# One decoder layer in fp32: transfers of the attention turns issued by slots, and an eighth block-product pair

## The reference

```
h = rms_norm(x, g_pre_mix)
cb, cc, ch, q, k, v, ga, gb = split(h @ w_in)     # 512 x 6, then 1024 x 2 columns
y_a = (cb * causal_dwconv(cc * ch)) @ w_a
o = stick_breaking(q, concat(k_past, k), concat(v_past, v), sb_bias)   # 8 heads of 64
y_b = o @ w_b
x = x + rms_norm((sigmoid(ga) * y_a + sigmoid(gb) * y_b) @ w_o, g_post_mix)
```

## Time and profile before

| what | us |
|---|---|
| median of three runs | 1709.57 |
| the profiled execution | 1707.09 |
| its span, first to last instruction | 1705.4 |
| PE busy | 1659.8 |
| DVE busy | 1177.9 |
| ACT busy | 828.0 |
| POOL busy | 361.3 |

### The profile page before, as it was taken

How to read it: one execution, slowest core, us unless ns; L and a number is a source line. 1 busy time by engine, 2 the same in 40 slices (tenths; PEclk the granted TensorE clock), 3 DMA queues, 4 the chain that set the end, 5 groups by cost and what they waited for, 6 DMA issues and landing times.

```text
span 1705.4 us, 25989 instructions
## 1 busy us (share of the span) xinstructions
PE 1659.8 (97%) x8721; PEld 1428.5 (84%) x8721; DVE 1177.9 (69%) x1669; ACT 828.0 (49%) x1430; POOL 361.3 (21%) x292
## 2 busy tenths in 40 slices
PE   9899998989999999999999999999999999999998
PEld 8688887978788889998878888888888888888886
DVE  7865525636366355665878888888888698777566
ACT  7322245747466455224564444444444444465675
POOL 1244300000000000000126666666665100000100
PEclk9899999999999999999999999999999999999999
DMA  5112233222213412444322222222221863244333
GB/s 179 47 43 76 93 100 90 73 78 68 85 53 100 165 58 102 154 142 154 110 69 80 78 77 78 77 77 78 77 78 57 284 234 100 82 149 172 121 128 118
DMA packets 180042, 178.33 MB, mean 105 GB/s; under 512 B 17999, under 2 KB 144811, under 8 KB 179948
## 3 DMA queue, kind: packets, MB, share of 16 engines
q1 hardware_dynamic: 167706, 170.54, 30.8%
q10 hardware_dynamic: 12242, 6.58, 1.3%
HBM read 133.56 MB, written 43.52 MB: 104 GB/s over the span
## 4 chain that ended last, share of the span: by engine, by line
PE 68%; DVE 1%; ACT 1%; SPq 1%; issue 0%; DMA 0%; POOL 0%; DVEq 0%; ACTq 0%; POOLq 0%
PE pair L3729 10%; PE pair L3789 8%; PE pair L3791 8%; PE pair L3790 8%; PE pair L3927 4%; PE pair L3928 4%; PE pair L3929 4%; PE pair L3798 2%; PE pair L3222 2%; PE pair L3272 2%; PE pair L3274 2%; PE pair L3273 2%; PE pair L3199 2%; PE pair L3197 2%; PE pair L3198 2%; PE pair L3592 1%
## 5 line engine op out<-in xcount | busy, mean ns | idle before, releaser
L3272 PE MATMUL pair<-xh,wh 128*128 128x384 f32 (+1 forms) x600 | 208.2, 347 | 1.1 <-DVE kl L2542 1.1
L3274 PE MATMUL pair<-xh,wl 128*128 128x384 f32 (+1 forms) x600 | 198.1, 330 | 0.0
L3273 PE MATMUL pair<-xl,wh 128*128 128x384 f32 (+1 forms) x600 | 198.1, 330 | 0.0
L1249 POOL TENSOR_TENSOR hn<-hn 128x512 f32<-128x512 f32 x4 | 5.2, 1292 | 646.0 <-DVE hn L2751 646.0
L3927 PE MATMUL pair<-woph,foph 128*128 128x512 f32 x308 | 120.4, 391 | 0.0
L3929 PE MATMUL pair<-woph,fopl 128*128 128x512 f32 x308 | 119.9, 389 | 0.0
L3928 PE MATMUL pair<-wopl,foph 128*128 128x512 f32 x308 | 119.9, 389 | 0.0
L3272 PEld LDWEIGHTS pair<-xh,wh 128*128 128x128 f32 x600 | 115.3, 192 | 4.9 <-issue 3.2
L3273 PEld LDWEIGHTS pair<-xl,wh 128*128 128x128 f32 x600 | 114.8, 191 | 0.0
L3274 PEld LDWEIGHTS pair<-xh,wl 128*128 128x128 f32 x600 | 114.5, 191 | 0.0
L1761 ACT ACTIVATE keep<-pair,bias 128x512 f32<-128x512 f32 (+4 forms) x100 | 58.2, 582 | 66.1 <-DVE pair L2601 42.0
(11 more groups left out here) (534 smaller groups left out, 4860.1 us busy)
## 6 DMA issues: line engine op xcount, KB each, us to landing
rawp<-in_w_up SPq DMA_DIRECT2D x88, 256.0 KB, 3.8
wd<-in_w_down SPq DMA_DIRECT2D x55, 256.0 KB, 2.8
raw<-in_w_in SPq DMA_DIRECT2D x52, 256.0 KB, 3.4
f_spill<-cv SPq DMA_DIRECT2D x22, 552.0 KB, 2.8
f<-f_spill SPq DMA_DIRECT2D x44, 256.0 KB, 5.4
gat<-gate_spill SPq DMA_DIRECT2D x16, 544.0 KB, 4.5
x_spill<-x SPq DMA_DIRECT2D x16, 512.0 KB, 2.9
wraw<-in_w_in SPq DMA_DIRECT2D x28, 256.0 KB, 3.8
```

What stands on the lines that cost most here:

```text
L3272: t_.matmul(b, h, xhi, start=(k == 0), stop=False, skip_group_check=True)
L3273: t_.matmul(b, h, xlo, start=False, stop=False, skip_group_check=True)
L3274: ins = t_.matmul(b, l, xhi, start=False, stop=(k == KD - 1), skip_group_check=True)
```

## The change

1. The last turn has four gate tiles instead of six. The two gate tiles that leave it become an eighth wide pair ("g", 2), and "g", 1 moves from the last place to the fifth.
2. `k_twice` on ACT is replaced by two DMAs from SBUF to SBUF, issued by SP (`keys_twice`). PE waits for them before the first scores of a turn.
3. The DMAs of rows, of attention output and of the samples leave ACT's queue and stand in SP's. SP's order in a turn is no longer by tiles, but by slots.
4. `new_rows` stands after the second piece of its slot and no longer at the slot's end.
5. In the opening, ACT copies block b and the samples before the two last high parts of sums; DVE makes the low parts of pair 1 before `convolve(0)`; POOL begins pair 1's sums when all four sums of x are done.

```diff
-TURN_GATES = (2, 2, 2, 6)
+TURN_GATES = (2, 2, 2, 4)
-WIDE_PAIRS = [("g", 0), ("c", 1), ("b", 0), ("c", 2), ("c", 3), ("b", 2), ("g", 1)]
+WIDE_PAIRS = [("g", 0), ("c", 1), ("b", 0), ("c", 2), ("g", 1), ("c", 3), ("b", 2), ("g", 2)]
...
+            def rows_out(c, kind, g):
+                hold(a_m, evacs.step())
+                if kind == "k":
+                    src, o, os_, sm = stg[g][:, :].rearrange("p (b n) -> p b n", n=P), kp_o, ks_o, stg_out[g]
+                else:
+                    src, o, os_, sm = vn[c % 2][:, 3 * g:3 * g + 3, :], vp_o, vs_o, vn_out
+                nb = 3 if g < 2 else 2
+                sp.dma_start(o[:, 3 * g:3 * g + nb, ds(c * P, P)], src[:, 0:nb, :]).then_inc(sm, 16)
...
+            def keys_twice(c):
+                hold(a_qk, 1 + 2 * NG * (c + 1))
+                for h in range(2):
+                    t = ks2[c % 2][h]
+                    sp.dma_start(f(t)[other(h), 0:SEQ], f(t)[own(h), 0:SEQ]).then_inc(k2_in, 16)
...
             keys(0, 3)
             load(in_job(5))
+            keys_twice(0)
+            load(in_job(6))
+            for gr in range(NG):
+                rows_out(0, "k", gr)
             for q in range(4):
                 values(0, q)
-            load(in_job(6))
             load(in_job(7))
             for c in range(NC4):
...
+                for n in range(SLOTS):
+                    unit_, kind, gr = ended_in(c, n)
+                    if gr == 0:
+                        j = TURN_JOB[c] + unit_ // NG + 3
+                        if j < IN_JOBS:
+                            load(in_job(j))
...
+                    if n and rows_after(c, n - 1):
+                        rows_out(c + 1, *rows_after(c, n - 1))
+                    if n and ended_in(c, n - 1)[1:] == ("k", NG - 1):
+                        keys_twice(c + 1)
+                    if n in OUT_AT:
+                        head_out(c, OUT_AT[n])
+                    if c + 1 < NC4:
+                        if n == 0:
+                            hold(p_past, 4 * c + 4)
+                            keys(c + 1, 0)
+                            keys(c + 1, 1)
+                        if n == STATE_SLOT + 1:
+                            hold(p_x, 4 * c + 4)
+                            for q in range(4):
+                                values(c + 1, q)
+                        if n in PAST_AT and PAST_AT[n] < 2:
+                            hold(p_past, 4 * c + 4 + PAST_AT[n] + 1)
+                            keys(c + 1, 2 + PAST_AT[n])
...
+                    if kind == "g":
+                        gate_out(JOBS[TURN_JOB[c] + unit_ // NG][1], gr)
@@ POOL, wide_sums(1)
-                    pool.wait_ge(p_x0, 2 * NBK)
+                    pool.wait_ge(d_ws, 4)
@@ ACT, the opening
                     plain("a")
-                    sum_high(2, 3)
                     plain("b")
                     wide_sc(0)
+                    sum_high(2, 3)
                     sum_high(3, 4)
@@ ACT, the turns
-            def k_twice(c):
-                act.wait_ge(a_qk, 1 + 2 * NG * (c + 1))
-                for h in range(2):
-                    s_.activation(ks2[c % 2][h][other(h), 0:SEQ], f(ks2[c % 2][h])[own(h), 0:SEQ], ACT.Copy)
...
-                act.wait_ge(a_m, mis.at())
-                o, os_, sm = (kp_o, ks_o, stg_out[g]) if kind == "k" else (vp_o, vs_o, vn_out)
-                nb = 3 if g < 2 else 2
-                act.dma_start(o[:, 3 * g:3 * g + nb, ds(c * P, P)], dst[:, 0:nb, :]).then_inc(sm, 16)
@@ DVE, the opening
             sum_low(2)
-            sum_low(3)
...
-            dve.wait_ge(a_m, 1)
-            convolve(0)
+            sum_low(3)
             wide_h(1, 0)
             wide_b(1)
             sample_sum(0)
             wide_c(1)
+            dve.wait_ge(a_m, 1)
+            convolve(0)
@@ PE, the turns
                     if j == 1:
                         pe.wait_ge(d_qk, qkn.at(2 * NG - 1))
+                        pe.wait_ge(k2_in, 32 * (c + 1))
...
+                        if i == first_piece(c, n) + 2 and rows_after(c, n):
+                            new_rows(c + 1, *rows_after(c, n))
...
-                    if rows_after(c, n):
-                        new_rows(c + 1, *rows_after(c, n))
```

More of the change, by code:

```diff
@@ L586, in build @@
         g_in = [g_mix_in, g_up_in, sem("g_ple_in")]
-        gains_in = sem("gains_in")
+        gains_in = sem("k2_gains_in")
         p_in = sem("o_out_p_in")
@@ L695, in build @@
         o_out, P_IN0 = p_in, 48 * (NC4 - 1)
+        k2_in, GAINS0 = gains_in, 32 * NC4
         p_pages = sem("p_pages")
@@ L899, in values @@
                 cached(c, q, range(4 * q, 4 * q + 4), lambda q, i: pv[:, 4 * q + i, :], cvv, pv_in)
-            def gate_out(m):
-                for g in range(NG):
-                    o, w = GROUPS[g]
-                    hold(a_gt, NG * (m - WIDE_GATES) + g + 1)
-                    sp.dma_start(gate_spill[m:m + 1, :, o:o + w].rearrange("o p t -> p (o t)"), stg[g][:, 0:w]).then_inc(stg_out[g], 16)
             def ab_job(m):
@@ L912, in ab_job, with gate_out, head_out, sample_out @@
                 return parts
+            def gate_out(m, g):
+                o, w = GROUPS[g]
+                hold(a_gt, NG * (m - WIDE_GATES) + g + 1)
+                sp.dma_start(gate_spill[m:m + 1, :, o:o + w].rearrange("o p t -> p (o t)"), stg[g][:, 0:w]).then_inc(stg_out[g], 16)
+            evacs, samples = Count(), Count()
+            evacs.base = M0
+            def rows_out(c, kind, g):
[6 more added lines that the diff above has]
+                sp.dma_start(o[:, 3 * g:3 * g + nb, ds(c * P, P)], src[:, 0:nb, :]).then_inc(sm, 16)
+                if g == 2:
+                    sp.dma_start(os_[:, ds(c * P, P)], src[0:NS, 2, :]).then_inc(sm, 16)
+            def head_out(c, i):
+                half = STEPS[VALUES[i][0]][0]
+                hold(a_m, evacs.step())
+                if c + 1 < NC4:
+                    sp.dma_start(o_spill[c:c + 1, :, CW * half:CW * half + CW].rearrange("o p t -> p (o t)"), ot[:, 0:CW]).then_inc(o_out, 16)
+            def sample_out(c):
+                hold(a_x, 1 + samples.step())
+                if c + 1 < NC4:
+                    sp.dma_start(o_spill[c:c + 1, :, SEQ:TOK].rearrange("o p t -> p (o t)"), ot[:, CW:CW + NS]).then_inc(o_out, 16)
+            def keys_twice(c):
[3 more added lines that the diff above has]
+                    sp.dma_start(f(t)[other(h), 0:SEQ], f(t)[own(h), 0:SEQ]).then_inc(k2_in, 16)
             hold(p_wq, W_END)
@@ new lines, in _ @@
+                for n in range(SLOTS):
[4 more added lines that the diff above has]
+                            load(in_job(j))
+                        elif j < IN_JOBS + 2:
+                            load(ab_job(j - IN_JOBS))
+                    if c == 0 and n == 0:
+                        rows_out(0, "v", 0)
+                    if c == 0 and n < NG - 1:
+                        rows_out(0, "v", n + 1)
+                    if n and rows_after(c, n - 1):
[4 more added lines that the diff above has]
+                        head_out(c, OUT_AT[n])
+                    if c + 1 < NC4:
+                        if n == 0:
[9 more added lines that the diff above has]
+                            keys(c + 1, 2 + PAST_AT[n])
+                    elif n == 1:
@@ L1726, in out_in @@
                 evac(lambda b: [(dst, b[:, :])], avn.at(2 * i + 2), ob_)
-                if c + 1 < NC4:
-                    act.wait_ge(a_m, mis.at())
-                    act.dma_start(o_spill[c:c + 1, :, CW * half:CW * half + CW].rearrange("o p t -> p (o t)"), dst).then_inc(o_out, 16)
             def sample_in(c):
@@ L1771, in slots @@
                         natural(c + 1, *rows_after(c, n - 1))
-                    if n and ended_in(c, n - 1)[1:] == ("k", NG - 1):
-                        k_twice(c + 1)
                     if not last and n - 1 in PAST_AT:
@@ L2141, in gate_high @@
                 act.wait_ge(gate_in[k], GATE_IN0[k] + 16)
-                act.wait_ge(gains_in, 16)
+                act.wait_ge(gains_in, GAINS0 + 16)
                 then(s_.activation(raw_, raw_, ACT.Copy, scale=gains[:, k:k + 1]))
```

30 lines of the change are left out of this document (2 added, 28 removed).

## The result

The changed kernel took 1684.88 us (median of 4 runs, 1684.70 to 1688.32) against 1708.69 (1707.41 to 1711.85) of the kernel before, run beside it: ratio 0.9863, 95% interval 0.9844 to 0.9882. The forecast was 1683 with a range of 1675 to 1695. The profiled execution took 1684.9 against 1707.1, which is -22.2 where the sum said -25.0.

The account below looks back on a forecast made before the run. PE, busy 97% of the span, was taken as the bound, its long waits paid twice through a halved clock. Terms summed to -25.0 from 1707.1, giving 1682.1 us profiled; the forecast was set at 1683, range 1675 to 1695.

Parts of the forecast that it names:

- the `pk` waits with their clock: Turns 0 to 2: issuing `pk` copies earlier removes three PE waits (10.3 us) and three half-rate stretches (5.9), -16.2 together.
- the k rows: PE's three waits for `stg`: taking one DMA issue off ACT's chain saves 0.45 us each, -1.4, bounds 0 and -4.6.
- the term of the last turn: Fewer pieces make slots 0.9 us shorter, so PE newly waits for DVE's steps: +2.5 us, lower bound 0, upper 13.
- start of turn 0: The 3.5 us `beta` wait shrinks by 2.5, its half-rate stretch (1.7) and a row's DMA (0.3) go: -4.5.
- two tiles for a pair: Two plain gate tiles (23.8 us) become one wide pair (21.4): -2.4 us, give or take 0.2.
- opening: Before pair 1, one wait of about 6.5 us replaces the `wsb` and `wadl` waits: -3.0 us, bounds -6 and 0.
- The slower rival: In slots 13 to 18, v copies hold up raw weights and rows, costing 10 us a turn: 1720 us, chance 0.03.
- The rival of a chain of steps in the last turn: Last-turn waits grow longer and drop the clock, +8 us instead of +2.5: 1688.5 us, chance 0.18.

## Why the prediction was right, and where its terms were off

The step that carries it, the `pk` waits with their clock, was right in mechanism and size, and so was the total. Two places that cost 2 and 1 us were in no term, the k rows were put 0.4 too small, and the term of the last turn is right in its number more than in its working. In profiled time:

| term | predicted | measured | from |
|---|---|---|---|
| `pk` waits and their clock | -16.2 | about -16.3 | waits 10.3 and three stretches gone; 5.5 a turn when put back |
| start of turn 0 | -4.5 | -4.2 | `beta` wait 3.5 to 1.0, one stretch gone |
| raw weights of tile 7 | none | +2.0 | PE's wait of 1.1, stretch 300.36 to 303.77 (1.7), less 0.8 of waits for `stg` and `beta` that PE, coming later, does not have |
| waits for `stg` | -1.4 | -1.8 | 1.5 to 0.9 each, turn 0 as without that stretch |
| two tiles for a pair | -2.4 | -2.4 | 23.8 and 21.4 |
| opening | -3.0 | -3.0 | pair 1 starts 3.5 earlier, 0.5 lost inside it |
| last turn | +2.5 | +2.5 | 23.8 of tiles gone, 21.3 of time |
| feed-forward part | none | +1.0 | a wait of 0.8 for `adl` at 866 |
| sum | -25.0 | -22.2 | |

The rows of the table are read from checkpoints and from the lists of waits; their sum is the measured -22.2, but a split of the turn between two neighbouring terms is good to some 0.5 only (turn 0 gained 1.5, not 2.0, with tile 7's weights first). For the last turn the run with six gate tiles gives 1.8 instead of 2.5.

*Start of turn 0.* The prediction said that in the new order "the raw weights are issued before the v copies and land in time". For tile 6 that holds: ACT no longer waits there. The weights of tile 7 were left behind the copies in the same list of three lines, and ACT wanted them in turn 0 some 20 us later. The slower rival was to decide where a use is less than 18 us behind its issue. Here it is 21 us from the place ahead of the copies (272.10) to the moment ACT was ready (293.07), and it was still 0.9 late: behind the copies (17.3) come the issue of the weights themselves and their landing, 289.51 to 293.98, 4.5 us, which the rival's 18 left out. It named the place, and I set it against "three tiles ahead, that is 40 us" without following one load to its use. With 3 x 10 us its price was far off: the queue ran late once, and by as little.

*The k rows.* The term was mis-sized: one DMA on ACT was put at its idle time of 0.45, and the run with the rows on ACT shows 0.6 twice and 0.9 in turn 0. The idle time holds the issue (0.38) already. What it leaves out is the overlap of two neighbours on ACT: without the DMA, `wT` begins 0.37 behind the beginning of the copy to `stg` (398.98, 399.35), which takes 0.49; with it, 0.95 behind (400.36, 401.31). The difference is 0.58. The further 0.3 of turn 0 stays open.

*The opening.* Right as a sum and in its parts nearly: the single wait 6.8 (said 6.5), 1.6 lost to the clock (said 2.5; half of the stretch fell inside the wait), 0.5 at the samples' product. How much of the stretch falls inside the wait is luck: in the other two profiles of this opening that are named below PE lost 2.5 and 2.8.

*The tiles and the last turn.* They cancel, as the sum had it (-2.4 and +2.5), and the run without them is level. The rival of a chain of steps in the last turn falls: the waits there are short (0.67, 0.29, 0.45 the longest), with the clock at 1.00 throughout. But they add up to 1.5 only, where 2 to 3 were forecast: 0.67 at the first step (said 0.6), 0.29 at step 8 (said 0.9), 0.1 around steps 14 to 16 (said about 1), and 0.45 at the last but one, which was not named. The rest of the 2.5 stands in no wait, and the agreement of the number is in part luck.

*The feed-forward part* was not looked at. The wait for `adl` is 0.6 to 1.4 in the profiles of eleven runs besides, and absent before and in the run with six gate tiles; its cause stays open.

## What to carry to other kernels

A wait that a queue's order makes is removed by moving the issue to where its buffer comes free, and it pays twice when it is long enough to lower TensorE's clock; but every item that the moved group now stands in front of has to be followed to its own use, one by one, and "fetched tiles ahead" is no answer for the last one. Where one wait turns into a single later one, look at which operands the first products really need: here most of the last 10 us of gain were in putting small results that others wait for (a samples' sum, a bank's copy) ahead of large ones that nobody needs yet. Where an engine is slowed by its neighbour, moving the neighbour's work brought nothing, since both places lay on the same queue in front of the same wait.

## What was not expected of the hardware

The granted clock fell to 0.50 (1.2 GHz) at 300.36 us behind two short waits, 1.1 and 0.7 us, with 1.2 us of small score matmuls between them; in the run with the rows on ScalarE two single waits of 2.1 and 1.8 us passed with the clock at 1.00, and in the run with the second copy of k on ScalarE so did the same two waits, 1.1 and 0.7. So neither the length of the longest wait nor the pattern of the waits alone told where the clock would fall. The stretches also shift from run to run of one opening: 71.66 to 78.49, 73.24 to 80.06 and 70.69 to 80.93 in three profiles with the same opening and the same wait of some 6.8 us (changed kernel, six gate tiles, tile 7 first). TensorE worked at half rate for 3.2, 4.9 and 5.6 us of them, which makes up to 1.2 us of difference, more than several of the edits here.

GpSimd and VectorE slow each other by amounts that both rows show: a subtraction on GpSimd took 1.3 us alone and 3.2 beside VectorE's low part, which went from 2.28 to 3.36. In the changed kernel GpSimd's row runs from 67.69 to 70.87. VectorE's row that had begun before it (67.46) took its usual 2.29, and the one that began inside it (69.67) took 1.1 more. That reads as if each stood until the other's instruction was done and did not share; it is an inference from these rows, and no run was made to test it.
